# Scaling the attention probabilities on GpSimd instead of VectorE in a four-block hybrid kernel

## What is computed

```python
sc = jnp.einsum('bhqd,bhkd->bhqk', qblk, kh).astype(jnp.float32) * scale
sc = jnp.where(mask, sc, -jnp.inf)
p = jax.nn.softmax(sc, axis=-1)
return jnp.einsum('bhqk,bhkd->bhqd', p.astype(vh.dtype), vh)
```

## Time and profile before

| | |
|---|---|
| median of 3 runs | 1728.54 us |
| the profiled execution's own time | 1730.73 us |
| its span | 1728.9 us |
| granted TensorE clock | 0.99 |
| TensorE matmul busy | 1626.0 us (94%) |
| VectorE busy | 1010.5 us (58%) |
| ScalarE busy | 731.5 us (42%) |
| GpSimd busy | 46.7 us (3%) |

### The profile page before, as it was taken

One profiled execution on the slowest core, in us unless ns is written; L12 is line 12 of the kernel. 1 busy time (PEld: TensorE's weight loads), 2 busy tenths in 40 slices (PEclk: granted clock), 3 DMA queues, 4 the chain that ended last, 5 costly groups with the idle time before them and its releaser, 6 DMA issues.

```text
span 1728.9 us, 21488 instructions
## 1 busy us (share of the span) xinstructions
PE 1626.0 (94%) x8009; PEld 1327.5 (77%) x8009; DVE 1010.5 (58%) x2246; ACT 731.5 (42%) x1511; POOL 46.7 (3%) x48
## 2 busy tenths in 40 slices
PE   3999999999998999999999999999889989998998
PEld 3878777787776878777787877898757779985676
DVE  3397757443443478657443344576876554778663
ACT  3443543333333353544332424434456553354661
POOL 0000002000000000002000000000000000000000
PEclk9999999999999999999999999999999999999999
DMA  5322212233233233112223323332211223311121
GB/s 181 91 86 86 57 47 70 76 94 95 88 97 90 80 87 97 53 46 74 74 74 109 95 88 111 87 87 65 62 31 62 86 83 92 89 47 46 37 74 61
DMA packets 81386, 136.22 MB, mean 79 GB/s; under 512 B 8694, under 2 KB 34052, under 8 KB 81284
## 3 DMA queue, kind: packets, MB, share of 16 engines
q1 hardware_dynamic: 78244, 129.62, 25.2%
q10 hardware_dynamic: 3040, 5.24, 0.9%
HBM read 132.74 MB, written 2.10 MB: 78 GB/s over the span
## 4 chain that ended last, share of the span: by engine, by line
PE 43%; DVE 13%; ACT 4%; issue 2%; POOL 0%; ACTq 0%; DVEq 0%
PE gemm_bank L699 33%; PE aux_bank L753 3%; PE aux_bank L782 3%; DVE w_lo L1309 2%; PE aux_bank L770 2%; DVE rope L1401 1%; ACT w_hi L1004 1%; DVE head_sums L1354 1%; PE aux_bank L671 1%; DVE probs L1457 1%; ACT probs L1052 1%; DVE kT L1441 1%; PE aux_bank L741 1%; DVE probs L1469 1%; DVE product L1718 0%
## 5 line engine op out<-in xcount | busy, mean ns | idle before, releaser
L1309 DVE TENSOR_TENSOR w_lo<-raw,w_hi 128x512 fp32r<-128x512 f32 (+3 forms) x524 | 330.1, 635 | 474.3 <-ACT w_hi L1004 472.4
L1004 ACT ACTIVATE w_hi<-raw 128x512 fp32r<-128x512 f32 (+3 forms) x524 | 306.0, 587 | 710.7 <-PE gemm_bank L699 700.3
L699 PE MATMUL gemm_bank<-act_hi,w_hi 128*128 128x512 f32 x768 | 319.0, 415 | 16.5 <-DVE mq_flat L1342 5.3
L699 PE MATMUL gemm_bank<-act_hi,w_lo 128*128 128x512 f32 x768 | 301.1, 392 | 0.0
L699 PE MATMUL gemm_bank<-act_lo,w_hi 128*128 128x512 f32 x768 | 300.2, 391 | 0.0
L699 PE MATMUL gemm_bank<-w_hi,act_hi 128*128 128x384 f32 (+3 forms) x736 | 268.8, 365 | 6.4 <-DVE bq L1342 2.9
L699 PE MATMUL gemm_bank<-w_hi,act_lo 128*128 128x384 f32 (+3 forms) x736 | 257.2, 349 | 0.0
L699 PE MATMUL gemm_bank<-w_lo,act_hi 128*128 128x384 f32 (+3 forms) x736 | 257.1, 349 | 0.0
L699 PEld LDWEIGHTS gemm_bank<-act_hi,w_hi 128*128 128x128 f32 x768 | 145.0, 189 | 59.0 <-issue 14.6
L699 PEld LDWEIGHTS gemm_bank<-act_lo,w_hi 128*128 128x128 f32 x768 | 145.1, 189 | 31.3 <-issue 2.9
L699 PEld LDWEIGHTS gemm_bank<-act_hi,w_lo 128*128 128x128 f32 x768 | 144.7, 188 | 31.4
(11 more groups left out here) (285 smaller groups left out, 2128.8 us busy)
## 6 DMA issues: line engine op xcount, KB each, us to landing
raw<-in_w_in SPq DMA_DIRECT2D x104, 512.0 KB, 3.5
raw<-in_w_in SPq DMA_DIRECT2D x64, 384.0 KB, 3.3
raw<-in_w_out SPq DMA_DIRECT2D x32, 512.0 KB, 3.7
raw<-in_w_branch SPq DMA_DIRECT2D x24, 512.0 KB, 3.7
raw<-in_w_mem_kv SPq DMA_DIRECT2D x8, 512.0 KB, 3.7
raw<-in_w_in SPq DMA_DIRECT2D x16, 256.0 KB, 2.7
raw<-in_w_in SPq DMA_DIRECT2D x8, 416.0 KB, 4.0
x<-in_x SPq DMA_DIRECT2D x1, 2048.0 KB, 7.9
```

Source lines behind the costliest of these rows:

```text
L699: last = pe.matmul(o, a, c, start=begin and n == 0, stop=end and n == 2)
L1004: act.activation(w_hi[:, s % RING, 0:n], raw[:, p % RAW, kk % PIECE, 0:n], ACT.Copy)\
L1309: dve.tensor_tensor(w_lo[:, s % RING, 0:n], raw[:, p % RAW, kk % PIECE, 0:n], w_hi[:, s % RING, 0:n].bitcast(F32), ALU.subtract).then_inc( ...
```

## The change

The reciprocal stays on VectorE and signals a new semaphore, `row_inv_ready`. The multiplication of both heads' rows moves to GpSimd, which walks the same units in the same order, waits for the reciprocal of each, and signals `probs_scaled` after the second head. VectorE no longer waits for its own reciprocal. TensorE's wait is for the same semaphore as before.

```diff
@@ -1460,17 +1461,9 @@
         def scaled(a, m):
 
-            c, keys = a.column(m), a.kind(m).n_keys(m % NT) * P
+            c = a.column(m)
             dve.wait_ge(probs_ready, 2 * (a.first_unit + m + 1))
-            mark(dve.reciprocal(row_inv[:, c:c + 2], row_sum[:, c:c + 2]))
-            settle()
-            for x in range(2):
-                rows = probs[a.where][m % 3][:, x, 0:keys]
-                ins = dve.tensor_scalar(rows, rows, row_inv[:, c + x:c + x + 1], None, ALU.mult)
-                if x:
-                    ins.then_inc(probs_scaled, 1)
-                else:
-                    mark(ins)
+            dve.reciprocal(row_inv[:, c:c + 2], row_sum[:, c:c + 2]).then_inc(row_inv_ready, 1)
@@ -1976,6 +1969,19 @@
+        def scale_probs(a):
+
+            for m in range(len(a.units)):
+                c, keys = a.column(m), a.kind(m).n_keys(m % NT) * P
+                pool.wait_ge(row_inv_ready, a.first_unit + m + 1)
+                for x in range(2):
+                    rows = probs[a.where][m % 3][:, x, 0:keys]
+                    ins = pool.tensor_scalar(rows, rows, row_inv[:, c + x:c + x + 1], None, ALU.mult)
+                    if x:
+                        ins.then_inc(probs_scaled, 1)
+                    else:
+                        mark(ins)
+
@@ -1985,6 +1991,7 @@
             pool.wait_ge(sums_ready, 3 * l + 2)
             factors(mean_var[:, :, 1], 0, NT, 1.0)
 
+            scale_probs(attention_1(l))
             pool.wait_ge(yb_lo_ready, MH // 2 * (l + 1))
@@ -2007,6 +2014,7 @@
             factors_x(before + NMEM // P + 2 * NT)
+            scale_probs(attention_2(l))
```

More of the change, by code:

```diff
@@ L405, in hybrid_kernel @@
     heads_ready = sem("heads_ready")
+    row_inv_ready = sem("row_inv_ready")
     probs_scaled = sem("probs_scaled")
```

## The result

The changed kernel takes 1796.2 us (median of four runs, 1795.5 to 1797.5), beside 1728.6 for the kernel before on the same chip: a ratio of 1.039, 95% interval 1.0377 to 1.0403. It is slower by 67 us. I had forecast 1736 and a range to 1750: the sign was right, the size wrong by far. The profiled execution took 1796.5 us.

The account below looks back on a forecast made before the run. TensorE was taken to bound the kernel, so VectorE's work counts only where TensorE waits. Direct waits 12.5, less 9.2 relief, plus 3.9 contention gave +7.2 us: 1737.9 for the profiled execution, 1736 on the median, range 1725 to 1750.

Parts of the forecast that it names:

- What bounds the kernel: TensorE, occupied 94% of the span; VectorE's work matters only where TensorE waits, mainly in the second block's attention.
- The price on GpSimd: Multiplication at 1.25 ns per added column: 0.83, 0.67, 0.51 us for 512, 384, 256 columns.
- Term 1: Attention units where TensorE waits for scaled rows, or has little slack, get them later: 12.5 us lost.
- my 18 units: Units whose scaled rows weight loads already awaited, 21.1 us: ten of 512 keys, two of 384, six of 256; 11.8 us more.
- My list of slack: Next candidates: units 15 and 31, slack 0.43 us, lose 0.7 in all; 256-key units have 0.59 or more, enough.
- Term 2: VectorE's shorter queue gives time back in the second block's attention: 4.6 us per layer, 9.2 for both.
- Term 3: GpSimd is held beside VectorE's two-input residues: 0.39 us in each of ten waiting 512-key units, 3.9 us; VectorE not held.
- GpSimd is slow: Rival: multiplications run at the `zc` gain's rate, 2.1 ns per added column; +21.7 us, 1750; chance 0.12.
- above 1.2 us without company: Sign that the forecast is wrong: GpSimd's 512-column multiplications last over 1.2 us with no two-input work beside them.
- VectorE held as well: Rival: a residue or rotation starting during a GpSimd multiplication waits for its end; +12 us, 1740.7; chance 0.13.
- Fast: Rival: GpSimd multiplies at the clearing's 0.88 ns per column, and the shorter queue outweighs lateness; 1724 us; chance 0.13.
- no meeting: Rival: VectorE and GpSimd do not hold each other up in attention; +3.3 us, 1731.8; chance 0.20.

Follow-up runs that it names:

- run at the assumed price: Changed kernel, but GpSimd multiplies only the first 28, 92, 156 or 220 columns, so each instruction lasts as long as predicted: 1735.8 us.
- run with the long units alone: GpSimd scales only the 40 units of 384 and 512 keys, VectorE the other 56 as in the kernel before: 1778.6 us.
- pair of runs with and without it: Narrowed GpSimd multiplications, 1735.8 us; the same with VectorE also multiplying a constant mask into scratch after each reciprocal, 1743.0 us.
- delay runs: Changed kernel, no row scaled: GpSimd runs 4-column multiplications about as long as its pairs, then signals TensorE; two lengths, 1806.9 and 1790.9 us.
- the tails: Against the kernel before, GpSimd scales only columns from 256 on of 384- and 512-key units, starting at the reciprocal, with its own semaphore: 1729.3 us.
- the first units: GpSimd scales columns from 256 on of long units, plus the first unit of every pair of heads whole (20 of 128 keys, 4 of 256): 1726.8 us.
- started late: GpSimd scales 128-key units whole, and columns from 256 on of longer units only after VectorE signals the first 256: 1721.8 us, ratio 0.9955.
- contention alone: Kernel before, VectorE still scaling; after each reciprocal GpSimd multiplies 1 to 4 pieces of 256 constant-mask columns, for which nobody waits: 1734.6 us.
- diagonal matrix: No row multiplied: VectorE builds identity times reciprocals, and TensorE turns the rows by a product with it instead of a transpose: 1760.9 us.

## Why the prediction was wrong

**What bounds the kernel: right.** TensorE bounds it, and only its waits for the scaled rows and VectorE's queue count. The run without multiplication puts the whole stake at 17 us.

**The price on GpSimd: wrong, and the step that failed.** I took "1.25 ns per added column" from two instructions of 4 and 16 columns, and bounds of 0.88 and 2.1. Measured are 2.5 ns per column and 282 ns, so the excess over VectorE with the hand-over is 2.28, 1.77 and 1.27 us for 512, 384 and 256 keys, in place of 0.80, 0.61 and 0.43. The slope between two very narrow instructions said nothing of wide ones here, and neither did their fixed cost: by the measured line 4 columns would take 292 ns, and they took 193. The upper bound was none: it came from an instruction on another form of operand, and I let it stand as the worst case without a reason. The run at the assumed price came out at 1735.8 us, so this term accounts for the miss.

In this case's rows an fp32 TENSOR_SCALAR with a scalar per partition takes GpSimd 2.5 ns per column, against some 0.52 on VectorE (483 less 350 ns over 256 columns).

**Term 1, the direct waits: right in form, mis-sized by the price.** With the measured excess my 18 units give 10 x 2.28 + 2 x 1.77 + 6 x 1.27 = 34 us in place of 11.8. Those 18 units measured 36.9 us more, so the form holds. The measured increase of all the weight loads' waits is 70.9 us; the other 34.0 are units that had slack: of 256 keys with "0.59 or more of slack against 0.43", which 1.27 uses up, and the other long ones. Waiting are now 49, and the run with the long units alone shows that 49 of the 67 us sit in 40 units. This is why the loss grows faster than the price. My list of slack had a gap at its own price too: units 35 and 67, of 512 keys, had 0.31 and 0.34 us (at unit 35 the pair ends at 1211.71 and TensorE takes it at 1212.03), less than the 0.43 of units 15 and 31. With an excess of 0.80 that is about 1 us left out of the sum.

**Term 2, the relief: right in size, within wide bounds; its places are not shown.** Predicted 9.2 us; 7.2 measured in the pair of runs with and without it. In the changed kernel TensorE's waits for VectorE's `mq_flat`, `bv`, `kT` and `qT` fall from 12.7 to 1.5 us, which is about the 10.3 of less idle time elsewhere. But that is not shown to be the relief: TensorE itself comes later there, and VectorE waits for scores 110.7 us instead of 32.1. In the run without multiplication, where nothing is late, TensorE waits for `mq_flat` 5.3 us as before, so the 0.9 that term 2 took from `mq_flat` at unit 39 does not show as a shorter wait.

**Term 3, contention: right in kind.** GpSimd is held beside two-input work, 13.5 us in all: of its 192 instructions the 120 that have no TENSOR_TENSOR of VectorE beside them for more than 20 ns are within 10 ns of the undisturbed lengths. In the ten 512-key units that my 3.9 us were for, its pairs are 4.4 us over the undisturbed length in the changed kernel and 3.9 in the run at the assumed price. That the figure meets so well is partly luck: in that run the 3.9 us are not 0.39 in each unit but run from nothing to 1.17. That VectorE is not held at all was wrong: L1310 is at 643 ns in the mean against 635 before, which hides single residues of 1.06 us instead of 0.69 (unit 15). All in all VectorE's other work takes 10.1 us longer than without any multiplication.

**Not in the sum: the clock.** Behind longer idle spells the granted clock was lower in the changed kernel: 0.50 from 190 to 194, after the 3.66 us at unit 3, and from 1265 to 1270, after the 5.87 us at unit 39. The matmuls are occupied 17.8 us longer, of the 65.8. In the run at the assumed price the profiled execution had a clock of 0.992 and matmuls of 1621 us; but it was the fastest of ten, and the others had 0.986 to 0.990, against 0.990 in the profile of before. So there the clock cost little, though not always nothing.

**The rivals.** "GpSimd is slow" was the right mechanism, with 0.12, at 1750 us; with the true rate, the newly waiting units and the clock it would have been far beyond. The sign of "above 1.2 us without company" is the one that came true. "VectorE held as well" did happen, but not as I had put it: in unit 15 the residue lost 0.37 us and did not wait for GpSimd's end, and in the delay runs the same loss comes without VectorE being held. "Fast" and "no meeting" are ruled out by the lengths.

## What to carry to other kernels

Before moving work to another engine, take its price from an instruction of the same form and width, or treat the price as open upwards; here two narrow instructions gave neither the slope nor the fixed cost. Then list the slack of every unit against that price: units with slack can move for nothing (0.14% here), and each that has none pays in full and pulls the following stage with it. If two engines share a job, try letting the second start when the first has signalled, not at the same moment. With both starting together the tails gave nothing (1729.3 us, and 1726.8 with the first units, as these alone); started late, with the 128-key units, they gave 1721.8 us.

## What the runs showed of the hardware

- An fp32 TENSOR_SCALAR with a scalar per partition took GpSimd 602, 922, 1242 and 1562 ns for 128, 256, 384 and 512 columns, undisturbed in the changed kernel.
- VectorE's one-input multiplication was longer with GpSimd's multiplications beside it: 256 columns took 458 in place of 350 ns on average (contention alone). With the tails neither engine stood still through the other's whole instruction at unit 3: VectorE's pair started at 184.53 and ended at 185.37, and GpSimd's first instruction of that unit ran from 184.58 until its second began at 185.65. One after the other they would need 0.62 and 0.92 us, 1.54 in all; both were over within 1.12, so they ran in part at the same time.
- A VectorE residue with two SBUF inputs that started while a GpSimd multiplication of 512 columns ran took 1.06 us instead of 0.69 (unit 15), and GpSimd's pair kept its 3.10 us. GpSimd's instruction beside VectorE's rotations took 3.11 us instead of 1.56 (unit 39).
- At unit 3 of the changed kernel, around and after the 3.66 us in which its weight loads stood still, TensorE's granted clock was 0.96 from 186 to 190, 0.50 from 190 to 194, 0.68 from 194 to 198 and 1.00 from 198 to 202.
- An fp32 product with a 128x128 matrix in place of a transpose was two loads of 191 ns and two matmuls instead of one load of 142 ns and one matmul (diagonal matrix, 928 of each against 464).
